# A transformer block with experts and a second block with a recurrent branch, on one core: where the experts' rows are made, and the order of the last stage

## The reference

```python
# first block: the router chooses two of 32 experts per row
x = x + gt1 * jnp.matmul(merged, w_out[l])
h2 = rmsnorm(x, norm2_g[l]) * (1.0 + sc2) + sh2
...
order = jnp.argsort(expert)             # 2048 rows by expert
tok = order // TOP_K_INNER
xs = h[tok]
a = lax.ragged_dot(xs, w1, sizes); b = lax.ragged_dot(xs, w3, sizes)
y = lax.ragged_dot(jax.nn.silu(a) * b, w2, sizes)
...
# second block, its end
x = x + rms_norm(hid @ w_down[l], g_ffn_post[l])                      # "n6"
ple_gate = jax.nn.sigmoid(rms_norm(x, g_ple_gate[l]) @ w_ple_gate[l])  # "n7"
ple = rms_norm(p[l].astype(x.dtype) @ w_ple_proj[l], g_ple_post[l])    # "n8"
x = x + ple_gate * ple
```

## Time and profile before

| | |
|---|---|
| median of 3 runs | 3521.37 us (3519.66 to 3521.44) |
| profiled execution | 3519.9 us, its span 3518.2 us |
| PE busy | 3193.8 us, 91% |
| DVE busy | 2194.6 us, 62% |
| ACT busy | 1312.0 us, 37% |
| POOL busy | 1008.7 us, 29% |
| DMA | 446.13 MB, mean 127 GB/s |

### The profile page before, as it was taken

One profiled execution on the slowest core, in us unless ns is written; L12 is line 12 of the kernel. 1 busy time (PEld: TensorE's weight loads), 2 busy tenths in 40 slices (PEclk: granted clock), 3 DMA queues, 4 the chain that ended last, 5 costly groups with the idle time before them and its releaser, 6 DMA issues. The chain is left out here.

```text
span 3518.2 us, 45077 instructions
## 1 busy us (share of the span) xinstructions
PE 3193.8 (91%) x15137; PEld 2535.4 (72%) x15137; DVE 2194.6 (62%) x2689; ACT 1312.0 (37%) x1717; POOL 1008.7 (29%) x513
## 2 busy tenths in 40 slices
PE   5889988888899599999959999699799999999988
PEld 4658866555677488888848788488578888888856
DVE  6588875687544799999865655643455145145285
ACT  3245423566412388888730364101221001000141
POOL 2323322000142011111124333244234444444442
PEclk9999999899999699999989999799899999999998
DMA  6313221231141799999961122032221111111312
GB/s 223 76 48 89 75 56 58 78 110 31 64 158 57 275 383 379 376 380 385 342 236 48 60 89 67 28 117 78 101 67 48 51 50 49 48 48 42 100 44 60
DMA packets 353122, 446.13 MB, mean 127 GB/s; under 512 B 33086, under 2 KB 237804, under 8 KB 353012
## 3 DMA queue, kind: packets, MB, share of 16 engines
q1 hardware_dynamic: 338308, 410.08, 34.3%
q10 hardware_dynamic: 5344, 17.83, 1.6%
q0 software_dynamic: 9360, 16.80, 1.3%
HBM read 397.40 MB, written 58.75 MB: 130 GB/s over the span
## 5 line engine op out<-in xcount | busy, mean ns | idle before, releaser
L410 PE MATMUL acc<-Ah,whi 128*128 128x512 f32 x2336 | 939.4, 402 | 80.2 <-DVE Al L604 20.5
L411 PE MATMUL acc<-Al,whi 128*128 128x512 f32 x2336 | 921.5, 394 | 0.0
L412 PE MATMUL acc<-Ah,wlo 128*128 128x512 f32 x2336 | 921.0, 394 | 0.0
L382 POOL TENSOR_TENSOR whi<-wraw,one 128x1024 fp32r<-128x1024 f32 (+3 forms) x214 | 391.9, 1831 | 1841.2 <-PE acc L412 1541.5
L410 PEld LDWEIGHTS acc<-Ah,whi 128*128 128x128 f32 x2336 | 445.6, 191 | 205.1 <-issue 74.3
L384 POOL TENSOR_TENSOR wlo<-wraw,whi 128x1024 fp32r<-128x1024 f32 (+3 forms) x214 | 536.1, 2505 | 16.8
L411 PEld LDWEIGHTS acc<-Al,whi 128*128 128x128 f32 x2336 | 445.8, 191 | 97.8 <-issue 6.2
L412 PEld LDWEIGHTS acc<-Ah,wlo 128*128 128x128 f32 x2336 | 445.1, 191 | 95.8
L1865 DVE TENSOR_TENSOR mlo<-mraw,mhi 128x1024 fp32r<-128x1024 f32 x256 | 307.0, 1223 | 45.7 <-ACT mhi L1812 32.2
L1812 ACT ACTIVATE mhi<-mraw 128x1024 fp32r<-128x1024 f32 x256 | 267.4, 1063 | 78.7 <-PE acc L1757 52.2
L410 PE MATMUL acc<-Bh,whi 128*128 128x512 f32 x640 | 250.8, 392 | 8.0 <-POOL wlo L384 8.0
(11 more groups left out here) (496 smaller groups left out, 4779.7 us busy)
## 6 DMA issues: line engine op xcount, KB each, us to landing
mraw<-in_exp_w SPq DMA_DIRECT2D x512, 256.0 KB
mraw<-in_exp_w SPq DMA_DIRECT2D x128, 512.0 KB, 12.0
wraw<-in_w_in SPq DMA_DIRECT2D x72, 512.0 KB, 3.8
wraw<-in_w_up SPq DMA_DIRECT2D x48, 512.0 KB, 3.9
TT<-in_ada_w SPq DMA_DIRECT2D x32, 512.0 KB, 3.9
TT<-gates SPq DMA_DIRECT2D x32, 512.0 KB, 4.7
wraw<-in_w_down SPq DMA_DIRECT2D x24, 512.0 KB, 3.6
adaraw<-in_ada_w SPq DMA_DIRECT2D x16, 512.0 KB
```

Of the source, the lines that this page charges most:

```text
L382: ch(pool.tensor_tensor(whi[:, r, 0:k, 0:m], wraw[:, r, 0:k, 0:m], one[:, 0:1].unsqueeze(2).broadcast_to([P, k, m]), ALU.mult))
L410: pe.matmul(o, whi[:, r, j, 0:m], ih[:, k0 + j, cols], start=(j == 0), stop=False)
L411: pe.matmul(o, whi[:, r, j, 0:m], il[:, k0 + j, cols], start=False, stop=False)
L412: last = pe.matmul(o, wlo[:, r, j, 0:m], ih[:, k0 + j, cols], start=False, stop=(j == k - 1))
```

## The change

- The eight rows' blocks are turned and made directly behind the choice of experts; slots and places follow. On PE all turnings stand ahead of the place products.
- For the first slot ACT makes all eight high parts before the high part of the rows.
- The weights of `plep` are loaded and split as two items of four tiles each instead of eight; the second split waits for `n6_sum`. PE's products of it are the same matmuls (`embedded`).
- The Newton step of n6 writes into the PSUM bank `XX`, and the scaling reads it there.
- The mean for n8 stands behind the third gate product instead of the second; sums and gates on DVE are dealt out anew; gates have three buffers instead of two; `result(m)` stands behind `gate_raw(m)` instead of `gate_raw(m + 1)`; PE turns tiles 5, 6 and 7 behind the last product.

```diff
--- before.py
+++ after.py
@@ -104,7 +104,7 @@
 
 ITEMS = [("iq", 4), ("keys", 1), ("dviwfl", 1), ("gates", 16), ("fv", 4), ("qkd", 12), ("proj", 16), ("wout", 8),
          ("pool", 4), ("rx", 8), ("g2", 16), ("rg", 4), ("pw_rg", 8), ("mix", 16), ("wo", 8),
-         ("ffn0", 24), ("ffn1", 24), ("ffn2", 24), ("plep", 8), ("pleg", 8)]
+         ("ffn0", 24), ("ffn1", 24), ("ffn2", 24), ("plep", 2), ("pleg", 8)]
 N0 = {}
 _at = 0
 for _name, _n in ITEMS:
@@ -588,12 +588,12 @@
-    def newton_step(dve, ch, tag, r, t):
+    def newton_step(dve, ch, tag, r, t, to=None):
-        ch(dve.scalar_tensor_tensor(r, t, 1.5, r, ALU.add, ALU.mult))
+        ch(dve.scalar_tensor_tensor(r if to is None else to, t, 1.5, r, ALU.add, ALU.mult))
@@ -1500,14 +1500,13 @@
             for c in range(b):
                 last = pe.matmul(o, onesb[:], rOb[:, c, :], start=(b == NB and c == 0), stop=(c == b - 1))
         last.then_inc(S("routed"), 1)
-        turn_block(2)
+        for b in range(2, NB):
+            turn_block(b)
         pe.wait_ge(S("routed"), 3)
         for c in range(2 * NB):
             last = pe.matmul(X[0][:, 0:2 * (SLOTS + 1)], PLACE[:, c, :], ROWAT[:, c, :, :].rearrange("p a s -> p (a s)"),
                              start=(c == 0), stop=(c == 2 * NB - 1))
         last.then_inc(S("routed"), 1)
-        for b in range(3, NB):
-            turn_block(b)
 
     @block.scalar
     def _(act):
@@ -1582,7 +1581,8 @@
         ch(dve.tensor_tensor(rOb[:], rO1[:], rO2[:], ALU.add))
         dve.sem_inc(S("chosen"), 1)
 
-        scaled_row(0)
+        for b in range(NB):
+            scaled_row(b)
         dve.wait_ge(S("routed"), 1)
         number, taken_by, after, before = (rNt[:, k, :] for k in range(4))
         ch(dve.tensor_copy(number, Y[:, HALF + NB * N_EXP:HALF + (NB + 1) * N_EXP]))
@@ -1621,8 +1621,6 @@
         ch(dve.tensor_tensor(PLACE[:], count_up(P), spread(pos, P), ALU.is_equal))
         dve.sem_inc(S("routed"), 1)
 
-        for b in range(1, NB):
-            scaled_row(b)
         dve.wait_ge(S("gap_exp"), 1)
         ch(dve.tensor_reduce(gw, grp, AX.X, ALU.add))
         ch(dve.tensor_scalar(norm, p2, 1.0, None, ALU.add))
@@ -1837,11 +1835,9 @@
-        for q in range(EARLY):
+        for q in range(UPS):
-        for q in range(EARLY, UPS):
-            high_up(0, q, first=True)
@@ -2414,7 +2410,10 @@
                         sp.dma_start(PR[:], A["p_2"][0, 0].rearrange("(b p) n -> p b n", p=P)).then_inc(S("p_in"), 16)
                     for b in ((), (), (), (0, 1), (2, 3), (4, 5), (6,), (7,))[m]:
                         sp.dma_start(X3[:, b, :], x3T[b * P:(b + 1) * P, :]).then_inc(S("x3T_in"), 16)
-                load_run(sp, N0["plep"], 8, lambda m: WPP[:, :, ds(m * P, P)], k=2)
+                for t in range(2):
+                    sp.wait_ge(w_lo, N0["plep"] + t - 1)
+                    sp.dma_start(wraw[:, t, :, :].rearrange("p (k m) n -> p k (m n)", k=2),
+                                 WPP[:, :, t * HALF:(t + 1) * HALF]).then_inc(w_land[t], 16)
                 load_run(sp, N0["pleg"], 8, lambda m: WPG[:, :, ds(m * P, P)])
 
         @block.gpsimd
@@ -2517,6 +2516,7 @@
+    TURNS = ((), (), (), (), (0, 1), (2, 3), (4,), (5, 6, 7))
@@ -2524,7 +2524,9 @@
 
     @block.gpsimd
     def _(pool):
-        split_run(pool, N0["plep"], 8, k=2)
+        split(pool, N0["plep"], 0, landed[N0["plep"]])
+        pool.wait_ge(S("n6_sum"), KD)
+        split(pool, N0["plep"] + 1, 1, landed[N0["plep"] + 1])
         split_run(pool, N0["pleg"], 8)
 
     @block.tensor
@@ -2541,22 +2543,36 @@
                 last = pe.transpose(p_banks[m % 2][:, b * P:(b + 1) * P], C[:, m, b * P:(b + 1) * P], ident[:])
             last.then_inc(S("out_turned"), 1)
 
+        def embedded(m):
+            t, i = m // 4, m % 4
+            if i == 0:
+                pe.wait_ge(w_lo, N0["plep"] + t + 1)
+            pe.wait_ge(acc_free[m % 2], take(m % 2))
+            for k in range(2):
+                for h in range(2):
+                    o, cols = acc[m % 2][:, h * HALF:(h + 1) * HALF], slice(h * HALF, (h + 1) * HALF)
+                    pe.matmul(o, whi[:, t, 4 * k + i, :], pTh[:, k, cols], start=(k == 0), stop=False)
+                    pe.matmul(o, whi[:, t, 4 * k + i, :], pTl[:, k, cols], start=False, stop=False)
+                    last = pe.matmul(o, wlo[:, t, 4 * k + i, :], pTh[:, k, cols], start=False, stop=(k == 1))
+            last.then_inc(S("embedded") if i < 3 else w_used, 1)
+
         pe.wait_ge(S("p_lo"), 2)
-        for m in range(2):
-            product(pe, N0["plep"] + m, m, pTh, pTl, 2, free=take(m))
+        embedded(0)
+        embedded(1)
         pe.wait_ge(S("n6_sum"), KD)
         add_mean(pe, TT[:, 2, :], True, True, "n6_mean")
-        product_run(pe, N0["plep"] + 2, 6, pTh, pTl, 2)
+        for m in range(2, KD):
+            embedded(m)
 
         pe.wait_ge(S("n6_root_used"), 1)
         product(pe, N0["pleg"], 0, Ah, Al, free=take(0), ready=(S("n7_lo"), 0), after=square_mean)
-        product(pe, N0["pleg"] + 1, 1, Ah, Al, free=take(1))
-        pe.wait_ge(S("n8_sum"), 1)
-        pe.wait_ge(S("n7_root_used"), 1)
-        add_mean(pe, S8, True, True, "n8_mean")
-        for m in range(2, KD):
+        for m in range(1, KD):
             product(pe, N0["pleg"] + m, m % 2, Ah, Al, free=take(m % 2))
-            for t in ((), (), (), (0,), (1, 2), (3,), (4, 5), (6, 7))[m]:
+            if m == 2:
+                pe.wait_ge(S("n8_sum"), 1)
+                pe.wait_ge(S("n7_root_used"), 1)
+                add_mean(pe, S8, True, True, "n8_mean")
+            for t in TURNS[m]:
                 turn(t)
 
     @block.scalar
@@ -2574,7 +2590,10 @@
-            act.wait_ge(w_used, N0["plep"] + m + 1)
+            if m % 4 == 3:
+                act.wait_ge(w_used, N0["plep"] + m // 4 + 1)
+            else:
+                act.wait_ge(S("embedded"), m - m // 4 + 1)
@@ -2607,9 +2626,9 @@
-            ch(act.activation(TT[:, m % 2, :], TT[:, m % 2, :], ACT.Sigmoid))
+            ch(act.activation(TT[:, m % 3, :], TT[:, m % 3, :], ACT.Sigmoid))
-            for t in ((), (), (), (0,), (1, 2), (3,), (4, 5), (6, 7))[m]:
+            for t in TURNS[m]:
@@ -2618,12 +2637,12 @@
-        newton_step(dve, ch, "n6", R6, TT[:, 3, :])
+        newton_step(dve, ch, "n6", R6, TT[:, 3, :], XX[:])
-                ch(dve.scalar_tensor_tensor(C[:, m, :], C[:, m, :], vec("g_ffn_post_2", m), R6, ALU.mult, ALU.mult))
+                ch(dve.scalar_tensor_tensor(C[:, m, :], C[:, m, :], vec("g_ffn_post_2", m), XX[:], ALU.mult, ALU.mult))
@@ -2635,28 +2654,46 @@
 
         def gate_raw(m):
             dve.wait_ge(w_used, N0["pleg"] + m + 1)
-            ch(dve.tensor_tensor(TT[:, m % 2, :], acc[m % 2][:], R7, ALU.mult))
+            ch(dve.tensor_tensor(TT[:, m % 3, :], acc[m % 2][:], R7, ALU.mult))
             dve.sem_inc(acc_free[m % 2], 1)
             dve.sem_inc(S("gate_raw4"), 1)
 
-        for p in range(1, 5):
+        def scaled(m):
+            ch(dve.scalar_tensor_tensor(PL[:, m, :], PL[:, m, :], vec("g_ple_post_2", m), R8, ALU.mult, ALU.mult))
+
+        def result(m):
+            dve.wait_ge(S("ple_gate"), m + 1)
+            ch(dve.tensor_tensor(PL[:, m, :], PL[:, m, :], TT[:, m % 3, :], ALU.mult))
+            ch(dve.tensor_tensor(C[:, m, :], C[:, m, :], PL[:, m, :], ALU.add))
+            dve.sem_inc(S("result"), 1)
+
+        for p in (1, 2):
             square_sum(p)
         newton_step(dve, ch, "n7", R7, TT[:, 2, :])
         dve.sem_inc(S("n7_root_used"), 1)
         gate_raw(0)
-        for p in range(5, KD):
+        for p in (3, 4, 5):
+            square_sum(p)
+        gate_raw(1)
+        for p in (6, 7):
             square_sum(p)
         dve.sem_inc(S("n8_sum"), 1)
-        gate_raw(1)
+        gate_raw(2)
         newton_step(dve, ch, "n8", R8, BG[:, 2, :])
-        for m in range(KD):
-            ch(dve.scalar_tensor_tensor(PL[:, m, :], PL[:, m, :], vec("g_ple_post_2", m), R8, ALU.mult, ALU.mult))
-            dve.wait_ge(S("ple_gate"), m + 1)
-            ch(dve.tensor_tensor(PL[:, m, :], PL[:, m, :], TT[:, m % 2, :], ALU.mult))
-            ch(dve.tensor_tensor(C[:, m, :], C[:, m, :], PL[:, m, :], ALU.add))
-            dve.sem_inc(S("result"), 1)
-            if m + 2 < KD:
-                gate_raw(m + 2)
+        for m in range(2):
+            scaled(m)
+            result(m)
+        scaled(2)
+        gate_raw(3)
+        result(2)
+        for m in range(3, KD):
+            if m > 3:
+                gate_raw(m)
+            if m == 3:
+                scaled(m)
+            result(m)
+            if m + 1 < KD:
+                scaled(m + 1)
 
     @block.sync
     def _(sp):
```

## The result

The changed kernel takes 3488.36 us (median of 4 runs, 3485.6 to 3490.84), the kernel before 3520.51 beside it (4 runs, 3515.91 to 3521.44): a ratio of 0.9914, 95% interval 0.9903 to 0.9926, or about 30 us less (26 to 34); the two medians stand 32.2 apart. The forecast was 3491, 29.5 us under that median of before; the time lies in its own range. Run again later, beside another kernel, it was 3486.63 against 3518.86: 0.9906 (0.9890 to 0.9923).

The account below looks back on a forecast made before the run. PE, busy 91% of the span, was taken as the bound. Terms 3.3 + 5.3 + (6.6 + 3.0) + (4.5 + 3.0 + 0.9) + 4.0 = 30.6 us off 3519.9, plus 1.5 for the median, gave 3491; own range 3485 to 3496, overall 3483 to 3502.

Parts of the forecast that it names:

- Experts: Experts' start: rows stored earlier let the first gather and PE's first product start earlier; 3.3 us, bounds -1 to 4.2.
- the saturated end: End of the experts: turns 18.10 us apart at DMA share 1.02, so the weight stream has almost no slack.
- Rival (a): Experts: the saturated stream, not PE, carries its first pass to the end; nothing gained or 1 us lost, 3494 to 3495; 14%.
- Up to the first gate product: Last stage's start: two small splits and the root in PSUM free DVE's scalings from POOL; 5.3 us, bounds 0 to 8.9.
- Mean: Eighth norm's mean behind the third gate product: PE's 6.6 us wait for DVE goes, plus 3.0 of low clock.
- Results in gate order: Last stage: a 4.5 us wait before a turn goes, plus 3.0 of low clock and 0.9 of one turn.
- rival (b): Last stage: POOL's splits hold DVE ahead of gate 3, PE waits, or the 5.3 don't come; 3496 to 3502; 13%.
- Tail: Behind the last product: result 6 and tile 7's scaling leave the chain, the sigmoid stands open; net 4.0 us, bounds 3.2 to 5.0.
- The Trainium skill's fixed cost: DVE's scalings: 120 cycles with a PSUM source against 58 with SBUF; by this rule the sum would be 0.5 us smaller.
- exclusive lock: DVE against POOL: whoever starts first holds the other; POOL's splits hold DVE instructions with two SBUF inputs, 2.91 us for 1.28.

Follow-up runs that it names:

- the holds: Changed kernel with the first slot's four down pieces, or only the last two, issued once the first gather has landed: 3485.3 and 3489.3 us.

## Why the prediction was right, step by step

- **Experts, 3.3 (bounds -1 to 4.2): 3.7.** The chain of starts held: rows done at 1161.5 (1162.6), weights issued at 1170.6 (1171.7), index at 1180.5 (1182.0), where 0.6 of each is an earlier choice. The step that was mis-sized is the gather, taken at 5.9 with 7.4 as its upper bound: it was 7.65, above the bound, as the four down pieces stood in the queues (4.5 with them held). PE's first product came 3.6 us earlier, and without the earlier choice 3.0, against 4.2. Then I took 0.9 off for the saturated end, and instead 0.7 was added: the second turn stands 17.65 behind the first (18.02 before), and at the end three turns stand about 18 apart (17.96, 18.09, 18.03), where before it was four (18.01, 18.07, 18.10, 17.95). That 3.3 comes so near to 3.7 is luck in part, as the two misses cancel. Rival (a), the stream takes it all back, is refuted by 608.15 with the experts alone. But the holds show that the stream does limit the second slot.
- **Up to the first gate product, 5.3 (0 to 8.9): 5.8**, the size right, the reason half right, and so the agreement in part luck: the root's place alone, which the step rests on, would have given 0.5. That the scaling runs free with its root in PSUM is shown. The other half, PE waiting for the first gate's own weights, was in the trace as a stop of 3.1 us ahead of product 0, put down to "issue", and I did not follow it to POOL's split. DVE did lose the 8.9 to contention (its ten instructions from 3355.96 on took 21.4 us, and 12.6 at their lengths alone), but PE could not have used them before that split. The third low part now begins 7.6 us earlier after the sixth mean, then meets the second big split (3.16 us) and ends 5.8 earlier. And behind it DVE sets the pace, not ACT as I wrote: in both traces the low parts after it stand 3.9 us apart, with DVE never idle between them up to the seventh.
- **Mean, 6.6 + 3.0 = 9.6: 9.2** by the experiment that undoes it.
- **Results in gate order, 4.5 + 3.0 + 0.9 = 8.4: 5.9** by its own undoing. The wait was right; behind it 3.0 us of work ran at the low clock in this experiment (1.5 lost), and 6 in the kernel before, and a new wait of 1.5 stands against it. In this small form rival (b) came: POOL's splits held DVE in results 1 and 2 (2.8 to 3.3 us an instruction), gate 4 came at 3447.7, and ACT's copy stood behind its sigmoid. I had stepped DVE's queue against gate 3 (counted from the sixth mean it was done at 91.7, forecast 87.9, or 91.2 with two splits; PE needed it at 94.5, forecast 94.4), but not ACT's against the turnings' banks.
- **Tail, 4.0 (3.2 to 5.0): 4.3.**
- Parts of the last stage together: 22.1 of 23.3. From n7 to the last product it is 16.3, where the forecast's two parts gave 18.0; the new wait of 1.5 is about the shortfall. That stretch to n7 (5.8) and the two undoings (9.2 and 5.9) add up to 20.9 only; in the undoings less work ran at the low clock (3.9 and 3.0 us) than behind the same waits in the kernel before (some 6 each). All parts by stretches: 30.1 of 30.6.
- **The Trainium skill's fixed cost** of a PSUM source ("VectorE: DVE Perf Modes", TRN2 errata) is not seen: with POOL idle the scaling takes 1.27 to 1.28 us with its root in PSUM and 1.28 to 1.29 with it in SBUF. Its exclusive lock between DVE and POOL ("SBUF — State Buffer", Who interferes with whom) agrees with the held rows above: the two scalings in SBUF began 0.66 and 0.07 us after a split, and ended 1.1 us behind it.

## What to carry to other kernels

When two engines are both late at one place, removing one cause alone gives little (0.5 and 1.6 us here, of 5.8 for both); follow a stop marked "issue" to what ended just before it. After an order is changed, step the queues of all engines at each shared buffer, not only that of the engine that was moved. And compare stretches between fixed instructions: here the last stage repeats within 0.1 us and the experts within 0.9, where whole runs spread over 5.9; and a stretch that nobody touched moved by 3.7.

## What the runs showed of the hardware that was not expected

- The stretch between experts and last stage, identical code in all kernels, takes 1583.9 to 1584.2 us in ten traces and 1586.3 to 1587.5 in four. The changed kernel had 1587.4 and 1587.5, its twin with ACT's old order 1584.0. In all traces the granted clock falls to 0.50 at the same eight places (one of the four long traces has a ninth), and the spells add up to 95.5 us in the ten short ones, to 102.3 in the two of 1586.3 and 1586.6, and to 109.1 in the two longest. At 2240 the clock was low for 10.2 us in the two longest and in the kernel before, and for 3.4 in all others; the two longest have two more spells that are 3.4 longer. In the second trace of the changed kernel, and at the same place in its twin:

```profile
2239.90:2250.10 10.20, 6.26 (x14) 4.53 (x15) 7.38 (x6) 1.99 (x2) 4.23 (x4) 0.50 0.20 58
```
```profile
2239.80:2243.20 3.40, 2.90 (x6) 1.82 (x6) 3.07 (x4) 0.00 (x0) 1.06 (x1) 0.50 0.29 83
2243.20:2250.00 6.80, 5.75 (x25) 4.80 (x26) 4.14 (x4) 2.12 (x2) 0.85 (x2) 1.00 0.15 45
```

The length of a low spell at the same place in the same code thus varies from trace to trace. What decides it stays open: the long stretch of the changed kernel begins at 1756.98 and the short one of its twin at 1756.95. Both traces of the changed kernel are long, but they are of executions of 3490.16 and 3490.59 us, and of its six other executions, which have no trace, five took 3484.96 to 3488.2 and one 3490.84; that speaks against the kernel as the cause.
- A gather of one slot's rows takes 4.5 us when the four down pieces are held back and 7.65 with the weights streaming beside it.
